# A 256-token hybrid decoder layer in split fp32 on one core: doubled activation scratch, and softmax probabilities turned through VectorE and DRAM

## What is computed

```python
h = h + 0.5 * swiglu(rmsnorm(h, ffn1_norm), ffn1_w_gu, ffn1_w_down)      # D_FF = 2816
h = h + hybrid_mixer(rmsnorm(h, mix_norm), w_in, w_gk_up, b_gk, gla_out_norm, w_out, rel_bias)
h = h + 0.5 * swiglu(rmsnorm(h, ffn2_norm), ffn2_w_gu, ffn2_w_down)
ple_gate = sigmoid(rmsnorm(h, ple_norm) @ w_ple_gate)                   # p: 256 x 256
h = h + ple_gate * (p @ w_ple_proj)
return rmsnorm(h, final_norm)
# in the mixer, for each MoBA head:
probs = softmax(q @ k.T * scale + bias_tab[rel_bucket(distance)], causal)
o_m = probs @ v
```

## Time and profile before

| | |
|---|---|
| median of 3 runs | 537.82 us (537.56 to 539.17) |
| the profiled execution's own time | 537.52 us |
| its span, first to last instruction | 535.3 us |
| TensorE busy | 521.9 us (97%), 2475 matmuls |
| VectorE, ScalarE, POOL busy | 327.6, 271.9, 77.8 us |
| granted TensorE clock, mean | 0.996 of full speed |
| DMA | 112.02 MB, 209 GB/s in the mean |

### The profile page before, as it was taken

How to read it: one execution, slowest core, us unless ns; L and a number is a source line. 1 busy time by engine, 2 the same in 40 slices (tenths; PEclk the granted TensorE clock), 3 DMA queues, 4 the chain that set the end, 5 groups by cost and what they waited for, 6 DMA issues and landing times.

```text
span 535.3 us, 6918 instructions
## 1 busy us (share of the span) xinstructions
PE 521.9 (97%) x2475; PEld 424.1 (79%) x2475; DVE 327.6 (61%) x434; ACT 271.9 (51%) x336; POOL 77.8 (15%) x144
## 2 busy tenths in 40 slices
PE   8999999999988999999999999999999999999994
PEld 5788888888776888877777788888888888888883
DVE  3683655845628474455799586656666557374675
ACT  4953354433616384876153766354533454453736
POOL 1503222222210210000000000222222222010000
PEclk9999999999999999999999999999999999999998
DMA  8995877859567968341245286777678757368202
GB/s 257 367 364 186 274 236 258 265 155 303 167 229 225 388 191 318 118 131 66 80 157 173 75 283 220 213 240 249 197 226 283 251 181 244 134 232 274 80 0 78
DMA packets 78166, 112.02 MB, mean 209 GB/s; under 512 B 5408, under 2 KB 51184, under 8 KB 78016
## 3 DMA queue, kind: packets, MB, share of 16 engines
q1 hardware_dynamic: 71472, 93.34, 53.2%
q0 software_dynamic: 6512, 18.32, 10.4%
q10 hardware_dynamic: 160, 0.07, 0.0%
HBM read 103.82 MB, written 9.45 MB: 212 GB/s over the span
## 4 chain that ended last, share of the span: by engine, by line
PE 65%; DMA 18%; DVE 6%; issue 5%; ACT 3%; POOL 2%; SPq 0%; DVEq 0%; ACTq 0%; POOLq 0%
PE acc L545 60%; DMA act_in<-act_dram 8%; DMA act_dram<-act_sq 7%; PE side L545 3%; POOL act_in L488 2%; DMA raw<-in_ffn_w_gu 2%; PE turn L585 2%; ACT w_hi L909 2%; DVE w_lo L1195 2%; DMA h<-in_x 1%; DVE act_sq L1272 1%; DVE AT L1463 1%; DVE act L1262 0%; DVE w_lo L1496 0%; PE turn L545 0%
## 5 line engine op out<-in xcount | busy, mean ns | idle before, releaser
L1195 DVE TENSOR_TENSOR w_lo<-raw,w_hi 128x2048 fp32r<-128x2048 f32 (+1 forms) x87 | 192.1, 2214 | 60.9 <-ACT w_hi L909 60.8
L545 PE MATMUL acc<-w_hi,hT_hi 128*128 128x512 f32 x496 | 196.1, 395 | 0.2 <-DVE w_lo L1195 0.2
L545 PE MATMUL acc<-w_hi,hT_lo 128*128 128x512 f32 x496 | 193.3, 390 | 0.0
L545 PE MATMUL acc<-w_lo,hT_hi 128*128 128x512 f32 x496 | 193.2, 389 | 0.0
L909 ACT ACTIVATE w_hi<-raw 128x2048 fp32r<-128x2048 f32 (+1 forms) x87 | 160.0, 1851 | 30.5 <-PE acc L545 28.2
L545 PEld LDWEIGHTS acc<-w_hi,hT_hi 128*128 128x128 f32 x496 | 93.1, 188 | 21.9 <-issue 1.8
L545 PEld LDWEIGHTS acc<-w_hi,hT_lo 128*128 128x128 f32 x496 | 93.1, 188 | 19.6
L545 PEld LDWEIGHTS acc<-w_lo,hT_hi 128*128 128x128 f32 x496 | 93.2, 188 | 18.5
L950 ACT ACTIVATE a_hiT<-act_in 128x512 f32 (+1 forms) x22 | 13.9, 632 | 132.5 <-DMA act_in<-act_dram 132.5
L545 PE MATMUL acc<-w_hi,a_hiT 128*128 128x512 f32 x176 | 68.9, 391 | 3.1 <-DVE w_lo L1195 1.7
L545 PE MATMUL acc<-w_hi,a_loT 128*128 128x512 f32 x176 | 68.5, 389 | 0.0
(11 more groups left out here) (171 smaller groups left out, 340.6 us busy)
## 6 DMA issues: line engine op xcount, KB each, us to landing
raw<-in_ffn_w_gu SPq DMA_DIRECT2D x82, 512.0 KB, 5.0
raw<-in_ffn_w_down SPq DMA_DIRECT2D x40, 512.0 KB, 5.5
raw<-in_w_in SPq DMA_DIRECT2D x24, 512.0 KB, 6.5
act_dram<-act_sq POOLq DMA_DIRECT2D x22, 256.0 KB, 4.2
act_in<-act_dram POOLq DMA_DIRECT2D x88, 64.0 KB, 4.2
raw<-in_w_out SPq DMA_DIRECT2D x8, 512.0 KB, 4.3
raw<-in_w_ple_gate SPq DMA_DIRECT2D x8, 512.0 KB, 5.0
raw<-in_ffn_w_gu SPq DMA_DIRECT2D x10, 256.0 KB, 6.2
```

Source lines behind the costliest of these rows:

```text
L545: return nc.tensor.matmul(o, lhsT, rhs, start=start, stop=stop, skip_group_check=True)
L1195: V.tensor_tensor(w_lo[:, slot, :nk * N], raw[:, slot, :nk * N], w_hi[:, slot, :nk * N].bitcast(F32), ALU.subtract).then_inc(lo_ready, 1)
```

## The change

Four things are changed:

1. `act_in` and `act_dram` are doubled. POOL may write a block while the block before it is being read back, and waits for the block two before. ScalarE and VectorE split block b - 2 (no longer b - 1) at the end of block b; the last two blocks are split at units k = 1 and k = 3 of the down product. Blocks 1 and 2 stand outside the loop.
2. The probabilities are transposed as the activations are: at the end of `pr`, VectorE transposes a pair's six 128 x 128 pieces as 32 x 32 squares into `pr_sq`, POOL's queue writes them to `pr_dram`, waits, and reads them back in four pieces into `prT0` or `prT1` (`pr_turn`). The `pt` steps of TensorE (24 flips) and VectorE (8 copies from PSUM) are gone; pv reads `prT` through a pattern of 32-element runs. Before it writes `pr_sq` again, VectorE waits until the pair before is in DRAM.
3. `p` takes the way of the activations, as a 23rd block; its four flips are gone.
4. `MIX`, `ACT_STEPS` and `DVE_STEPS` are rewritten: each score step stands earlier, up to one behind the other.

The diff, cut to what the prediction speaks of:

```diff
     (40, 1): ["D7", "T_g0"],
-    (40, 2): ["T_g1", "pt0.0"],
-    (40, 3): ["pt0.1"],
-    (41, 0): ["sc1.0", "sc1.1"],
+    (40, 2): ["T_g1", "sc1.0", "sc1.1"],
+    (41, 0): ["sc2.0", "sc2.1"],
     (41, 2): ["diag"],
     (42, 0): ["lv0"],
     (42, 1): ["pv0"],
-    (42, 2): ["pt1.0", "pt1.1"],
-    (42, 3): ["lv1"],
-    (43, 1): ["sc2.0", "sc2.1"],
-    (43, 2): ["pv1"],
-    (44, 0): ["lv2"],
-    (44, 1): ["pt2.0", "pt2.1"],
-    (44, 2): ["sc3.0", "sc3.1"],
-    (44, 3): ["pv2"],
-    (45, 0): ["lv3"],
-    (45, 1): ["pt3.0", "pt3.1"],
-    (45, 2): ["pvg0"],
-    (45, 3): ["pvg1"],
+    (42, 2): ["lv1"],
+    (43, 0): ["sc3.0", "sc3.1"],
+    (43, 1): ["pv1"],
+    (43, 2): ["lv2"],
+    (44, 2): ["pv2"],
+    (44, 3): ["lv3"],
+    (45, 1): ["pvg0"],
+    (45, 2): ["pvg1"],
     (46, 0): ["pv3"],
     (47, 2): ["T_o0"],
     (47, 3): ["T_o1"],
@@ -103,15 +98,15 @@
 ACT_STEPS = ["hi38", "nat0", "hi39", "z", "hi40", "nat1", "T_k0", "D0", "hi41",
-             "T_k1", "D1", "D2", "hi42", "D3", "D4", "sc0", "D5", "nat2", "D6", "D7", "T_g0", "T_g1", "hi43",
-             "sc1", "hi44", "nat3", "pv0", "hi45", "sc2", "pv1", "hi46", "nat4", "hi47", "sc3", "pv2",
+             "T_k1", "D1", "D2", "hi42", "D3", "D4", "sc0", "D5", "nat2", "D6", "D7", "T_g0", "T_g1",
+             "sc1", "hi43", "sc2", "nat3", "hi44", "hi45", "pv0", "sc3", "hi46", "pv1", "nat4", "hi47", "pv2",
              "hi48", "pvg", "pv3", "nat5", "groot", "hi49"]
-DVE_STEPS = ["lo38", "lr", "z", "lo39", "la", "lo40", "lo41", "sc0", "lo42", "pr0", "pt0.0", "clear", "pt0.1",
-             "Z0", "sc1", "diag", "Z1", "pr1", "lo43", "lv0", "pv0", "pt1.0", "pt1.1", "lv1", "lo44",
-             "Z2", "sc2", "lo45", "pr2", "pv1", "lv2", "Z3", "pt2.0", "pt2.1", "lo46", "sc3", "lo47", "pr3",
-             "pv2", "lv3", "lo48", "pt3.0", "pt3.1", "pvg", "pv3", "gg", "o_g", "lo49"]
+DVE_STEPS = ["lo38", "lr", "z", "lo39", "la", "lo40", "lo41", "sc0", "lo42", "pr0", "sc1", "clear",
+             "Z0", "pr1", "sc2", "diag", "Z1", "lo43", "lv0.0", "lv0.1", "pv0", "pr2", "lv1", "Z2", "sc3",
+             "lo44", "pr3", "lv2", "pv1", "lo45", "Z3", "pv2", "lo46", "lv3", "lo47", "lo48", "pvg", "pv3",
+             "gg", "o_g", "lo49"]
...
-        AT2 = at("AT2", 56, [P, GH, P])
+        AT2 = at("AT2", 75, [P, GH, P])
         pr = at("pr", 58, [P, 2, 3 * P])
-        prT = at("prT", 61, [P, 2, 3 * P])
+        pr_sq = at("pr_sq", 72, [P, 2 * 3 * P])
+        prT = [at("prT0", 61, [P, 2 * 3 * P]), at("prT1", 54.5, [P, 2 * 3 * P])]
         oT_hi = at("oT_hi", 64, [P, MH // 2, T], F32R)
         oT_lo = at("oT_lo", 68, [P, MH // 2, T], F32R)
...
                 pool.wait_ge(act_turned, g + 1)
-                if g:
-                    pool.wait_ge(act_back, 64 * g)
-                pool.dma_start(act_dram, act_sq[:]).then_inc(act_out, 16)
+                if g >= 2:
+                    pool.wait_ge(act_back, 64 * (g - 1))
+                pool.dma_start(act_dram[g % 2], act_sq[:]).then_inc(act_out, 16)
                 pool.wait_ge(act_out, 16 * (g + 1))
-                if g:
-                    pool.wait_ge(act_lo, g)
+                if g >= 2:
+                    pool.wait_ge(act_lo, g - 1)
                 for j in range(4):
-                    pool.dma_start(act_in[32 * j:32 * j + 32, :].rearrange("p (i e) -> p i e", i=4),
-                                   bass.AP(tensor=act_dram.tensor, offset=P * j, ap=[[N, 32], [32 * N, 4], [1, P]])
+                    pool.dma_start(act_in[32 * j:32 * j + 32, g % 2, :].rearrange("p (i e) -> p i e", i=4),
+                                   bass.AP(tensor=act_dram.tensor, offset=g % 2 * P * N + P * j,
+                                           ap=[[N, 32], [32 * N, 4], [1, P]])
                                    ).then_inc(act_back, 16)
             def h_turn(f):
...
                                    bass.AP(tensor=h_dram.tensor, offset=2 * P * j, ap=[[2 * N, 32], [64 * N, 4], [1, 2 * P]])
                                    ).then_inc(h_back, 16)
+            def pr_turn(pair):
+                pool.wait_ge(pr_turned, pair + 1)
+                pool.dma_start(pr_dram[pair % 2], pr_sq[:]).then_inc(pr_out, 16)
+                pool.wait_ge(pr_out, 16 * (pair + 1))
+                if pair >= 2:
+                    pool.wait_ge(turn_done, TURN[f"pv{pair - 2}"] + 1)
+                w = 6 * 32
+                for j in range(4):
+                    pool.dma_start(prT[pair % 2][32 * j:32 * j + 32, :].rearrange("p (i e) -> p i e", i=4),
+                                   bass.AP(tensor=pr_dram.tensor, offset=pair % 2 * P * 4 * w + w * j,
+                                           ap=[[4 * w, 32], [32 * 4 * w, 4], [1, w]])).then_inc(pr_back, 16)
...
-                    pe.wait_ge(probs_ready, 2 * pair + i + 1)
-                    turn_open(t)
-                    for k in range(3):
...
                     t = TURN[s]
-                    pe.wait_ge(turn_read, turned(f"pt{pair}.1"))
+                    pe.wait_ge(pr_back, 64 * (pair + 1))
                     pe.wait_ge(acc_read, 2 * B_WIN + 8)
                     turn_open(t)
                     for i in range(2):
                         c = slice((2 * pair + i) * MD, (2 * pair + i + 1) * MD)
                         o = turn[64 * i:64 * i + 64, t % 2, 0:T]
-                        mm(o, nat1[:, 0, c], prT[:, i, 0:T], True, False)
-                        ins = mm(o[:, P:T], nat1[:, 1, c], prT[:, i, T:T + P], False, True)
+                        pT = prT[pair % 2][:]
+                        mm(o, nat1[:, 0, c], view(pT, [[32, 2], [192, 4], [1, 32]], 96 * i), True, False)
+                        ins = mm(o[:, P:T], nat1[:, 1, c], view(pT, [[192, 4], [1, 32]], 96 * i + 64), False, True)
                     ins.then_inc(turn_done, 1)
                 elif s == "diag":
                     o = [side_open(f"diag.{hh}") for hh in range(2)]
...
-                    if j:
-                        act_part(f, b - 1)
+                    if j and not (isinstance(b, int) and b == 1):
+                        act_part(f, b - 2, (j + NB * f) % 2)
                 blk(0, 0)
-                with act_e.Fori(0, (NB - 1) // 2) as i:
+                for b in (1, 2):
+                    blk(b, b)
+                with act_e.Fori(0, (NB - 3) // 2) as i:
                     for j in range(2):
-                        blk(i * 2 + (1 + j), 1 + j, i)
+                        blk(i * 2 + (3 + j), 3 + j, i)
                 for n in range(2):
                     for k in range(6):
                         u = U_DOWN[f] + 6 * n + k
-                        if n == 0 and k == 2:
-                            act_part(f, NB - 1)
-                        if f == 1 and n == 0 and k == 2:
-                            t = TURN["p"]
-                            act_e.wait_ge(turn_done, t + 1)
-                            A(pT_hi[:], turn[:, t % 2, :].rearrange("p (c t) -> p c t", c=2), ACT.Copy).then_inc(turn_hi, 1)
+                        if n == 0 and k in (1, 3):
+                            b = NB - 2 + k // 2
...
-                elif s[:2] == "pt":
-                    pair, i, t = int(s[2]), int(s[4]), TURN[s]
-                    dve.wait_ge(turn_done, t + 1)
+                    pair = int(s[2])
+                    dve.wait_ge(probs_ready, 2 * pair + 2)
                     if pair:
-                        dve.wait_ge(turn_done, TURN[f"pv{pair - 1}"] + 1)
-                    V.tensor_copy(prT[:, i, :], turn[:, t % 2, 0:3 * P]).then_inc(turn_read, 1)
+                        dve.wait_ge(pr_out, 16 * pair)
+                    else:
+                        dve.wait_ge(side_done, SIDE["D7"][0] + 1)
+                    for i in range(2):
+                        ins = V.transpose(view(pr_sq[:], [[192, 4], [32, 3], [1, 32]], 96 * i),
+                                          view(pr[:, i, :], [[32, 4], [P, 3], [1, 32]]))
+                    ins.then_inc(pr_turned, 1)
                 elif s == "pvg":
                     for m in range(M):
```

More of the change, by code:

```diff
@@ L143, in plan_turns @@
                 add(s, who="act")
-            elif s[:2] in ("T_", "pt") or s[:2] == "pv" and s[:3] != "pvg":
+            elif s[:2] == "T_" or s[:2] == "pv" and s[:3] != "pvg":
                 add(s)
@@ L147, in plan_turns @@
     add("h2.1", 2)
-    add("p")
     add("h3.1", 2)
@@ L252, in build @@
         act_sq = at("act_sq", 48, [P, N])
-        act_in = at("act_in", 50, [P, N])
+        act_in = at("act_in", 50, [P, 2, N])
         h_sq = at("h_sq", 48, [P, 2 * N])
@@ L533, in _ @@
             pool.dma_start(masks[:], pair_masks).then_inc(masks_in, 16)
+            for pair in range(MH // 2):
+                pr_turn(pair)
             pool.wait_ge(unit_done, U_GU[1])
@@ L538, in _ @@
                 act_turn(NB + b)
+            act_turn(2 * NB)
             h_turn(1)
@@ L869, in _ @@
                 acc_free(B)
-                pe.wait_ge(turn_read, turned("p"))
```

(32 more changed lines are left out.)

42 lines of the change are left out of this document (19 added, 23 removed).

## The result

The changed kernel takes 531.61 us (median of 4 runs, 530.84 to 532.45), the kernel before 537.69 (4 runs, 535.87 to 539.17); the ratio is 0.9889, with a 95% interval of 0.9852 to 0.9926. In a second set (e5) it was 0.9876 (0.9855 to 0.9898), with a median of 530.84. The forecast was 531.5. The four times are 530.84, 530.86, 532.36 and 532.45: the median falls into a gap between two kinds of execution, which e5 looks at. The profiled execution took 530.84 us against 537.52, 6.7 less; its span is 528.8.

The account below looks back on a forecast made before the run. TensorE was taken as the bound, busy for 521.9 of 535.3 us. Terms of -5.7 us from the profiled 537.52 gave 531.8, and some 0.4 for fewer interruptions led to 531.5 us, range 529.4 to 534.8.

Parts of the forecast that it names:

- the sum: Whole kernel: -3.1 - 2.65 - 0.8 - 0.45 + 1.3 = -5.7 us.
- Part 1: First FFN's down product: the doubled scratch removes TensorE's waits for a_loT and w_lo, -3.1 us.
- the walk: First FFN: counting back from 164.4 puts the end of block 10's matmuls, and its silu's start, at 130.5.
- Part 2: Probabilities: 24 flips leave TensorE, -2.65 us; pt1's buffer wait behind oT_lo goes, -0.8; p's four flips go, -0.45.
- interruptions: TensorE's weight stream: five fewer interruptions by pt steps, 0.04 to 0.15 us each, some 0.4 us more gained.
- Part 3: Mixer's new order: TensorE waits 1.3 us in front of diag until VectorE has read sc2's scores, +1.3 us.
- The narrow places behind it: Mixer behind diag: lv1 holds by 0.7 us, sc3 and pvg0 with less than 1 us in hand.
- The trip: Probabilities' way through DRAM: back 11.6 us behind the squares, 14.7 if slow, with at least 15 there: 0 us.
- The rival in which it made the kernel slower: Probabilities' DRAM trip: trips of about 20 us make the pv steps wait 7.3 us together, 539.4 us; chance 5%.
- VectorE as the bound: Mixer: VectorE's list makes diag, lv1, sc3 and pvg0 each wait 1 us more, 535.5 us; chance 15%.
- The 3.1 us coming back elsewhere: First FFN: its stall only moves, to the down product's end or the mixer's first chunk, 534.6 us; chance 6%.

Follow-up runs that it names:

- e5: The changed kernel run once more, unedited, for its spread: median 530.84 us, 0.9876 of the kernel before.
- e1: The changed kernel with the scratch used as one buffer again and the splits back at block b - 1: 536.81 us, 0.9976 of the kernel before.
- e11: e4 with the scratch used as one buffer and the splits at block b - 1: 534.32 us, 0.9954 of the kernel before.
- e10: e4 run once more, unedited: 529.12 us, 0.9855 of the kernel before.
- e2: The changed kernel with the mixer of before (flips, PSUM copies, old tables); doubled scratch and p's new way stay: 533.26 us, 0.9912 of the kernel before.
- e7: The changed kernel with the splits back at block b - 1, both halves of the scratch still in use: 531.08 us, 0.9871 of the kernel before.
- e9: The changed kernel with the scratch used as one buffer, splits kept at block b - 2: 542.01 to 559.84 us, median 550.45.
- e3: The changed kernel with diag one chunk later in TensorE's list: 530.18 us, 0.9856 of the kernel before.
- e6: The changed kernel with diag one chunk earlier in TensorE's list: 534.32 us, 0.9928 of the kernel before.
- e4: The changed kernel with VectorE's clear and Z0 moved from in front of pr1 to behind sc2: 529.14 us, 0.9842 of the kernel before.
- e8: The changed kernel with one more DRAM to DRAM copy in the probabilities' round trip: 532.13 us, 0.9896 of the kernel before.

## Why the prediction was right

The time came out 0.1 us from the forecast, and that closeness is luck. No execution took 531.6 us: the median lies between two of 530.86 and two of 532.36 or more, and in the second set it is 530.84. Two sizes in the sum were off and partly made up for each other, and the clock, which the sum didn't have, made up for more. The mechanisms of the three parts are the ones that the runs show. In the profiled pair, between the marks, the 6.7 us are 3.7 ahead of T_g1 (part 1), 2.3 from there to T_o0 (parts 2 and 3 together), 0.5 behind it (`p`) and 0.2 outside the span.

- **Part 1, -3.1 us.** The mechanism was right: the window between 150 and 175 is full, and block 10's silu starts at 130.11 (130.5 in the walk, 137.60 before):

```profile
130.11 0.84 ACT L966 ACTIVATE silu_g<-acc,rstd 128x256 f32<-128x256 f32 x2 [3.52 <-PE acc L561]
```

The size was too small twice. TensorE's idle time isn't all that a wait costs: the 3.1 us idle were 16 matmuls, 3.6 us, in that same execution. And one profiled execution's stall was taken for the stall: the wait for `a_loT` is 1.4 us in one profile, 0.4 in another, 1.8 in e1's. In medians e11 and e10, and e1 and the changed kernel, both give 5.2, and e2 with the old mixer 4.5 (538.25 less 533.26, less 0.5 for `p`). That it is the DMA traffic which makes the trip of an execution long or short wasn't shown. "The place" and "the buffer" were one edit to me; e7 and e9 show that the buffer is all of the gain, and the place alone a loss of 4.5 us in its fastest execution and 22 in its slowest.
- **Part 2, -2.65, -0.8 and -0.45 us.** T_o0, the mark behind the mixer, starts at 298.96 instead of 304.95, 5.99 us sooner, and T_g1, ahead of the first change, 3.72 sooner. The mixer thus gave 2.27, and what lies ahead of it is part 1's. With the new wait (1.83) added and the two old ones (0.82 and the 0.14 us idle between 275 and 300) taken off, 3.1 us are the flips' and their interruptions': 2.65 and 0.4 in the sum. Behind T_o0 another 0.5 us went, `p`'s flips. The moving operand in runs of 32 has no price: eight pv matmuls take 0.81 us from the first's start to what follows, before and after. The two transposes of a pair take 1.04 us, 1.05 in the sum.
- **Part 3, +1.3 us.** The mechanism and the place were right, the size was 1.83. The term that was small is VectorE's: 8.1 us from the start of sc1 to its last score of sc2, where the trace has 240.21 to about 248.6, 8.4, and then 0.2 for the hand-over to TensorE. pr1, its transposes and sc2 are each 0.10 to 0.15 us longer, from start to start, than the terms taken for them. The narrow places behind it held, and e3 shows that lv1's margin was real: at 1.36 us less it waited 0.6.
- **What the sum didn't have** is the clock. Three of eight executions are 1.6 us longer at a lower mean clock. e1 and e6 show such a drop behind the wait in front of diag; e4 and e10, which haven't the wait, have no second kind.
- **The trip, 0.** Right, and for three of four pairs with more room than I gave it (7.1 to 8.6 us against 11.6; the last took 11.3); e8 lengthens it by 3.5 to 5.4 us without a wait. The rival in which it made the kernel slower falls. The mechanism that the Trainium skill offers for it (SBUF — State Buffer, "SBUF: two separate sides", the "DVE blocks DMA" trap) doesn't show: POOL's issues take 0.56 us beside VectorE's work in the mixer, as they do in the FFNs. In the changed kernel no issue meets a division of the probabilities; in e4 pr1's (242.34 to 243.77) runs beside pair 0's four reads, and they land in 2.4 to 2.6 us. No row shows whether the division runs in the fast mode that the page speaks of.
- **VectorE as the bound** was the right fear in one place of four. That a 128 x 128 transpose belongs on TensorE, as the Trainium skill has it (VectorE: DVE Perf Modes, "Rules for kernel authors"), doesn't hold in this kernel: e2, which keeps it there with the old order, is about 2 us slower than the changed kernel, and 4.1 slower than e4, in which VectorE's list is put in a better order. TensorE's time is nearly the whole span here, and VectorE still has a fifth of its own free in the mixer (busy for 48.88 of 60 us from 239 to 299).
- **The 3.1 us coming back elsewhere** didn't happen: the windows from 150 to 225 are full.

## What to carry to other kernels

Where one scratch buffer carries a round trip as long as the work that hides it, double the buffer before touching any list: here 127.3 us of in-order waits in front of it stayed and cost nothing. Count the missing matmuls of a stretch, not its idle time alone, and take a second profile before sizing a stall. To fit work between two engines, walk both lists from one hand-over to the next and look at what stands between the input's arrival and the result that the bound engine wants; moving 2.3 us of work that nobody waits for behind that result gave back 1.7 us, where moving the waiting step gave half of it and moved the wait on. And a stall of TensorE can cost more than its length: here 1.5 us more behind one of 1.8 us in one profile of six, and 2.5 more behind one of 3.2.

## What the hardware showed that wasn't expected

A wait of TensorE of 1.8 us was followed by a stretch at half clock in some executions: in e1's profile (1.5 us lost), but not in the five others that have this wait in front of diag (the changed kernel's, e5, e7, e8, e9); and three of the changed kernel's eight executions are 1.6 us longer with a mean clock of 0.993. One of 3.2 us was followed by a longer stretch: 0.50 from 250 to 254, and before and behind that in part, in e6, with all four executions at 533.8 us or more. e9's two waits at the down products, 2.9 and 3.7 us, have a drop each (0.93 and 0.86 over 25 us). The 0.8 us wait of the kernel before shows none. That the length of the wait decides is what these runs suggest, not a law: the kernel before waits 1.4 and 1.7 us close together in the first FFN, and its two profiles show no drop there, but four of its later executions have a mean clock of 0.993 or 0.994 as well, and where their clock fell isn't known.
